# Which queue brings the first weight tiles of a hybrid attention layer: four loads moved from SyncE's queue to ScalarE's

## The reference, cut to what matters

```python
def rms_norm(x, g):
    xf = x.astype(jnp.float32)
    y = xf * lax.rsqrt(jnp.mean(xf * xf, axis=-1, keepdims=True) + RMS_EPS)
    return (y * g.astype(jnp.float32)).astype(x.dtype)

    h = rms_norm(x, ln_attn_pre[l])
    mix = hybrid_mixer(h, w_in[l], ...)     # proj = h @ w_in, 2188 columns
    x = x + rms_norm(mix @ w_out[l], ln_attn_post[l])
    f = (jax.nn.silu(h @ ffn_w_gate[l]) * (h @ ffn_w_up[l])) @ ffn_w_down[l]
```

## Time and profile before

| | |
|---|---|
| three runs, us | 1224.31, 1224.70, 1227.16 |
| median, us | 1224.7 |
| the profiled execution's own time, us | 1224.95 |
| its span in the profile, us | 1223.1 |
| granted TensorE clock over the span | 0.998 |
| busy share of the span | PE 99%, DVE 70%, ACT 50%, POOL 15% |
| DMA queue q1 (SP) | 66596 packets, 135.67 MB |
| DMA queue q10 (ACT) | 144 packets, 0.26 MB |

### The profile page before, as it was taken

How to read it: one execution, slowest core, us unless ns; L and a number is a source line. 1 busy time by engine, 2 the same in 40 slices (tenths; PEclk the granted TensorE clock), 3 DMA queues, 4 the chain that set the end, 5 groups by cost and what they waited for, 6 DMA issues and landing times.

```text
span 1223.1 us, 18751 instructions
## 1 busy us (share of the span) xinstructions
PE 1205.3 (99%) x6586; PEld 1036.8 (85%) x6586; DVE 860.3 (70%) x1638; ACT 609.1 (50%) x1172; POOL 180.0 (15%) x153
## 2 busy tenths in 40 slices
PE   9999999999999999999999999999999999999997
PEld 7899788888999999888888888888888888888886
DVE  6423797968779765547966765756657568887888
ACT  5442787757677755434743333333333345544443
POOL 5230211111100000111001112201122021000014
PEclk9999999999999999999999999999999999999999
DMA  7303511137733000323213323133231356643443
GB/s 246 123 1 122 121 43 45 40 108 174 177 105 100 24 19 18 103 87 121 87 44 112 129 86 121 66 115 129 87 129 60 139 198 225 240 161 115 153 175 138
DMA packets 66834, 137.13 MB, mean 112 GB/s; under 512 B 8552, under 2 KB 27248, under 8 KB 66741
## 3 DMA queue, kind: packets, MB, share of 16 engines
q1 hardware_dynamic: 66596, 135.67, 34.7%
q10 hardware_dynamic: 144, 0.26, 0.1%
HBM read 90.52 MB, written 28.60 MB: 97 GB/s over the span
## 4 chain that ended last, share of the span: by engine, by line
PE 79%; DVE 9%; issue 4%; ACT 4%; DMA 3%; SPq 1%; POOL 0%; DVEq 0%; POOLq 0%; ACTq 0%
PE ps L2548 32%; PE ps L2578 14%; PE ps L1134 8%; PE ps L2492 4%; PE ps L1114 4%; PE ps L978 4%; PE ps L997 3%; PE ps L923 2%; PE ps L1079 2%; PE ps L1087 2%; PE ps L1012 1%; DVE ring L1515 1%; DMA m_qs<-m_qn 1%; PE ps L1145 1%; DVE m_rows_sb L1522 1%
## 5 line engine op out<-in xcount | busy, mean ns | idle before, releaser
L2548 PE MATMUL ps<-f_topH,f_W 128*128 128x512 f32 x704 | 220.7, 389 | 0.8 <-DVE f_W L2339 0.8
L2548 PEld LDWEIGHTS ps<-f_topH,f_W 128*128 128x128 f32 x704 | 132.1, 188 | 28.7 <-DVE f_W L2339 1.3
L2339 DVE TENSOR_TENSOR f_W<-f_scr,f_W 128x512 fp32r<-128x512 f32 (+1 forms) x128 | 89.8, 704 | 86.9 <-ACT f_W L2102 86.8
L2548 PE MATMUL ps<-f_topL,f_W 128*128 128x512 f32 x352 | 136.9, 389 | 0.0
L1134 PE MATMUL ps<-V,m_tw 128*128 128x66 f32 (+1 forms) x1056 | 127.8, 272 | 0.1
L2578 PE MATMUL ps<-f_headH,f_W 128*128 128x512 f32 x408 | 127.4, 389 | 0.5 <-DVE QT L2372 0.5
L1134 PEld LDWEIGHTS ps<-V,m_tw 128*128 128x128 f32 x1056 | 125.2, 192 | 2.6 <-DVE m_mix_n L1565 1.3
L2548 PE MATMUL ps<-f_headH,f_W 128*128 128x512 f32 x352 | 114.7, 390 | 0.0
L2102 ACT CAST f_W<-f_scr 128x512 fp32r<-128x512 f32 (+1 forms) x128 | 77.6, 610 | 30.0 <-PE ps L2578 15.7
L2578 PEld LDWEIGHTS ps<-f_headH,f_W 128*128 128x128 f32 x408 | 76.6, 188 | 16.7 <-issue 0.9
L2339 DVE TENSOR_TENSOR f_W<-ring,f_W 128x512 fp32r<-128x512 f32 x60 | 59.6, 1006 | 33.4 <-ACT f_W L2102 33.3
(11 more groups left out here) (283 smaller groups left out, 2644.0 us busy)
## 6 DMA issues: line engine op xcount, KB each, us to landing
act_pairs<-QT SPq DMA_DIRECT2D x77, 256.0 KB, 4.2
m_qs<-m_qn SPq DMA_DIRECT2D x128, 128.0 KB, 2.4
ring<-in_ffn_w_up SPq DMA_DIRECT2D x22, 512.0 KB, 3.7
f_stage<-act_pairs SPq DMA_DIRECT2D x40, 256.0 KB, 3.5
ring<-in_ffn_w_gate SPq DMA_DIRECT2D x19, 512.0 KB, 4.5
f_scr<-act_pairs SPq DMA_DIRECT2D x37, 256.0 KB, 3.3
ring<-in_ffn_w_down SPq DMA_DIRECT2D x11, 512.0 KB, 5.4
f_pair_up<-in_ffn_w_down SPq DMA_DIRECT2D x11, 512.0 KB, 6.8
```

What stands on the lines that cost most here:

```text
L2339: dve.tensor_tensor(slot_part(s, 1), source(s), slot_part(s, 0).bitcast(F32), ALU.subtract).then_inc(lo_done, 1)
L2548: ins = pe.matmul(ps[:, bank, :], whole[:, w, cols], halves[h][:, k0 + k, col:col + HALF], start=(begins and k == 0 and w == 0 and h == 0) ...
```

## The change

The four loads of weights leave SP's program and are issued by ACT, on its own queue, right behind its first load and ahead of its function table load. SP's queue begins with x alone. The number of warm-up products goes from 11 to 13.

```diff
-WARM_PRODUCTS = 11
+WARM_PRODUCTS = 13
...
             load_x(0)
             for k in range(1, 5):
                 load_x(k)
-                if k == 1:
-                    load(sp, "wf", 0)
-                if k < FIRST_TILES:
-                    load(sp, "wf", k)
             sp.dma_start(oh[0:32, :], onehot[0:32, :]).then_inc(ext_oh_in, 16)
...
             act.dma_start(ring[:, slot_of["wf", 0], 0:HALF], w_first[0][:, 0:HALF]).then_inc(consts_in, 16)
+            for k in range(FIRST_TILES):
+                load(act, "wf", k)
             act.preload_act_table_set("natural_log_exp_and_others")
```

## The result

The changed kernel takes 1227.76 us (median of 20 runs, 1224.46 to 1232.96), the kernel before 1224.23 (20 runs). The ratio on record is 1.0022, with an interval of 1.0014 to 1.0031: **slower by 0.22%, about 2.7 us**, a small difference that the runs do tell from none. The profiled execution took 1226.83 us with a span of 1225.0, which is 1.9 us more than before, at the same granted clock of 0.998. One run of the kernel before (1332.48 us) and the profiled execution of experiment 4 (3118.26 us) were disturbed and stand in no ratio, and of the latter's profile only the first loads are read.

What follows compares the result with a forecast made beforehand. PE is nearly always busy, so only the first 24 us, set by DVE's chain behind ACT, could change. Issues 0, gain 0, x 1 +0.08, warm-up 0 gave about +0.1 us: 1224.8 us, range 1222.8 to 1226.4.

Steps and rivals of the forecast that it cites:

- What bounds: The first 24 us: the end hangs on DVE's chain, set back by ACT; PE's waits there total 1.50 us.
- the number to watch: Start of `hidden_hi(1)` on ACT, 8.89 us before; POOL, DVE, PE from 23.83 and the end move with it; forecast 8.97.
- ACT's issues: Four more issues ahead of ACT's table load cost 1.7 to 3.0 us, hidden in its wait for the gain: 0.
- The rival that ACT is late: Slow issues and table load begin step 0 2.0 us late: 1226.0, or 1228.7 if the clock fell; chance 0.08.
- The gain's own landing: The gain on SP's queue, its small rows waiting behind weight rows, 0.3 us late, absorbed by ACT: 0.
- The second half of x 0: Loaded from 4.50 to 6.00 us, where a second queue takes little from the first; x 1 is late next.
- What ACT can absorb: Step 0 on ACT takes 2.91 us without waits, so may begin 0.73 us late with `cut_hi(1)` still at 8.36.
- x 1: Sharing the engines with weight load 1, it lands at 8.97 instead of 7.72 us: `hidden_hi(1)` +0.08 us.
- x falls behind further: Even sharing from the gain on: x 1 at 9.60, +0.71 us, 1225.4; with the gain's 0.63 us, 1226.0; chance 0.25.
- The warm-up: Two more products on PE cost 0.76 us at most and end at 5.99, ahead of the first product: 0.

Runs made afterwards that it cites:

- experiment 4: The changed kernel with weight load 1 as two loads with rows of 2 KB, same bytes: 1225.95 us, ratio 1.0005.
- number 1: The kernel before with 13 warm-up products instead of 11, loads unchanged: 1226.17 against 1224.91 us, ratio 1.0008.
- number 5: The kernel before with only the second half of weight load 0 moved to ACT, 11 warm-up products: 1223.40 against 1225.18 us, ratio 0.9981.
- number 10: The kernel before with the second half of weight load 0 and weight load 1 moved to ACT, 11 warm-up products: 1224.07 us, ratio 1.0000.
- number 12: The changed kernel once more, unchanged, for a second profile: 1227.43 us, ratio to the kernel before 1.0022.
- number 2: The changed kernel with 11 warm-up products instead of 13: 1227.28 us, ratio to the kernel before 1.0019.
- number 3: The changed kernel with the gain issued by ACT behind its first load, out of x's queue: 1225.62 us, ratio 1.0004.
- number 6: The changed kernel with six products of ones between the two halves of step 0 on PE: 1228.15 us, ratio 1.0026.
- 8: The kernel before with ACT issuing the gain first, then both halves of weight load 0, SP the rest: 1225.87 us, ratio 1.0014.
- number 7: The changed kernel with the gain's 4 KB loaded a second time ahead of x 0's second half: 1228.71 us, ratio 1.0037.
- 11: The kernel before with only weight load 0's second half moved to ACT, 11 warm-up products, run once more: 1223.51 us, ratio 0.9993.
- 9: The kernel before with weight load 0's second half on ACT and the gain ahead of x 0 on SP: 1225.51 against 1224.85 us, ratio 1.0005.
- second and third series: Follow-up kernels 5 to 8 and 9 to 12, each series run on one chip with the kernel before.

## Why the prediction was wrong

**What bounds: right.** The first 24 us decide, `hidden_hi(1)` is the number to watch, and in the profiled pair it moved ACT, POOL, DVE, PE's step 3 and the span by 1.99, 1.99, 1.96, 1.97 and 1.9 us. The later stretch kept its time. That step 3 moves by just as much is no rule, though: it held since `hidden_lo(3)` took 3.41 us in both, and in number 1 it took 1.27.

**ACT's issues: right.** Five issues from 0.74 to 3.19 us, the table load ended at 4.50 with its 1.28 us unchanged, step 0 began at 4.70 to 4.92 in the profiles of the changed order. The rival that ACT is late did not come.

**The gain's own landing: right.** It came 3.7 instead of 3.5 us after its issue, and ACT could absorb that. What was missed is what it costs the rows behind it on its queue.

**The second half of x 0: wrong, and this is the step that failed.** "There a second queue takes little from the first" was read from 197 GB/s between 4.50 and 6.00 with one queue. But that stretch wasn't the second half's. On 15 of 16 engines it was in by 5.15 us; 62 rows of 4 KB, those of x 1, began in the stretch and 20 of 2 KB. Six rows of x 1 that began at 4.4 to 4.7 us took 1.5 to 1.7 us each instead of 0.159, and one engine was late. The half rate that the prediction gave to "x's second half" alone was thus a misreading: alone, its rows passed every 0.08 us. With weights on the other queue the second half paid twice: the gain's 128 small rows ahead of it took their turns (its first row went at 4.3 to 4.4 us instead of 3.66), and then its own rows did. It landed at 6.7 to 8.3 us instead of about 6.3, on 15 engines at 6.6 to 6.9 instead of 5.15. The toll was put at nothing, and it is what x 1, behind it on the same queue, inherits.

**What ACT can absorb: right, even a little small.** In number 5, without a wait, step 0 takes 2.71 us on ACT (4.82 to 7.53) and not 2.91, so it is 0.93 us rather than 0.73. In three of four profiles of the changed order `cut_hi(1)` starts at 8.28 to 8.54, against 8.36 before: the late second half alone cost 0.2 us at most there, and number 10 shows the same in the time. In the first profile, with the late engine, it starts at 9.92.

**x 1: its own share right, what it inherits left out.** The sum gave it 1.25 us for a second queue of equal rows, and loads 2 and 3 beside it do cost 1.21 (8.38 in number 10, 9.59 in number 12). But the sum let x 1 begin as before. Already with load 1 alone beside what stands ahead of it, it lands at 8.38 instead of 7.69, 0.69 us later. Together x 1 was there at 9.45 to 9.70 us in three profiles and at 10.85 in the first, not at 8.97. It is the last wait ahead of `hidden_hi(1)` in all four (0.36, 0.55, 0.58 and 0.73 us), which came 0.6 to 0.8 us late in three, 2.0 in the first, and not 0.08. The rival "x falls behind further", with a chance of 0.25, named the mechanism's direction; its landing of 9.60 and its +0.71 us are what three profiles show, but the 1226.0 that it gave at most is under the measured time.

**The warm-up: wrong in size, of no weight.** The 13 products took 5.59 us and not 4.96, and ended at 6.62; in the changed kernel x was later than that anyway. Alone they cost nothing measurable (number 1).

**What stays open.** That the loads make the kernel slower is shown by numbers 2, 3 and 10; the size is explained in part. The four profiles of the changed order have step 3 at 24.39, 24.27, 24.56 and 25.80. That is 0.9 us on average later than before, and 1.7 later than in number 1, which has the loads of the kernel before; the runs say 2.7 (1.7 to 3.8). A late DMA engine, as in the first profile, puts step 3 another 1.4 us later than the other three (24.41 on average). But the timed runs have no trace, so how often it comes wasn't seen, nor why that engine began x's rows late, nor on which side of POOL `hidden_lo(3)` usually falls in the kernel before. A single profile's total can't help: from step 3 to the end the profiled executions take between 1198.0 us (number 2) and 1204.7 (number 6), more apart than the whole effect. What the medians of the second and third series do is rank as step 3 does in their profiles: 22.97, 24.10, 24.27 and 26.05 us go with 1223.40, 1225.87, 1228.15 and 1228.71 (5, 8, 6, 7), and 22.63, 23.06, 23.61 and 24.56 with 1223.51, 1224.07, 1225.51 and 1227.43 (11, 10, 9, 12).

## What to carry to other kernels

In this kernel a second DMA queue added no bandwidth where the first one's loads were due first: it took a turn for each of their rows, and the loads with the shorter rows lost most. What is late on a queue makes all that stands behind it late, so follow a delay down the queue before you call it absorbed. Put on the second queue only what is needed as early as the first queue's loads (here one or two weight loads cost nothing, four cost 2.7 us), and judge a dip in GB/s by whose rows it holds and by its last engine before you fill it. A tiny load with one small row to a partition took as many turns here as 512 KB of 4 KB rows: place it where nothing urgent stands behind it.

## What the runs showed of the hardware that was not expected

- Where both queues had rows waiting, they took turns row by row on a DMA engine, 2 KB for 84 ns and 4 KB for 159, whatever their size: 66 and 63 rows in a microsecond with 0.27 and 0.11 MB in the changed kernel, 65 and 65 with 0.14 and 0.26 in number 3, where the sizes are the other way round.
- Taking 4 KB out of x's queue (number 3) brought `hidden_hi(1)` back to 8.61 us, from 9.5 to 10.9 in the four profiles of the changed order. Putting 4 KB more into it (number 7) made the first row of the next load 1.4 us later.
- One of the 16 engines can be 1 to 1.6 us behind the others with the same loads (6.06 after 5.09, 8.32 after 6.72). In the kernel before, with its queue alone, it passed its rows every 0.08 us; beside another queue every 0.236.
- `hidden_lo(3)` on DVE took 3.41 us in the six profiles in which POOL's add had begun before it, by as little as 0.06 us, and 1.27 in the seven in which it began first, by as little as 0.04.
- The warm-up's pace was not the same from kernel to kernel: 11 products took 4.20 us before and 4.76 to 5.07 in six other profiles that differ only in DMAs; 13 took 5.20 to 5.77 in five profiles and 4.59 in that of number 3.
